# One-core three-branch block: where the first and third branch's merges take up their first gates

## The chip, the cores and the metric
The kernel runs on one core of one Trainium2 chip, as one launch. The metric is device time in microseconds (us). The three runs of the kernel before took 2590.54, 2594.08 and 2594.62 us, so its median is 2594.08 us.

## The reference, cut to what matters
The reference is a block of two layers on 512 tokens (256 of context, 256 of the sequence) with 1024 features, and then a second block of two layers on the 256 tokens of the sequence. Only the first block is touched. In each of its layers three branches read the same normalised input h: an mLSTM (a), a differential attention (b) and a Fourier mix (c). Each has a gate of its own, and their gated outputs are summed:

```
for l in (0, 1):
    h   = modulate(rmsnorm(x), c)
    y_a = rmsnorm(mlstm(h)) * sigmoid(o) * silu(z)      # 4 heads, 256 columns each
    y_b = attention(h) * silu(bz)
    y_c = fourier_mix(cu) * silu(cz)                    # 4 groups of 256 columns
    m   = sigmoid(mg_a) * (y_a @ w_a_out) + sigmoid(mg_b) * (y_b @ w_b_out) \
        + sigmoid(mg_c) * (y_c @ w_c_out)               # mg_* = h @ w_in[...]
    x   = x + gate * (m @ w_out)
```

`fourier_mix` of a group transforms its 256 columns (first transform) and then along its 256 tokens (second transform), each as a product with tables of cosines and sines. In layer 0 all 512 tokens go through; in layer 1 only the last 256 are needed at the end.

## The kernel before, in words
**Layout.** Activations lie with features on the 128 partitions and tokens along the free axis, in 8 tiles. Each tile is kept as a high part (rounded to fp32r) and a low part (the rest): `HYh` and `HYl`, whose first half is the layer's input H and whose second half is the branch's output YB. Weights are split in the same way, `wh` and `wl`. A projection of 128 output columns is 8 tiles times 3 matmuls (high*high, high*low, low*high), 24 matmuls in one PSUM bank, on 512 tokens in layer 0 and on 256 in layer 1.

**Weights.** They come in units of 256 columns, in a fixed order, one DMA each into a ring `raw` of 2. ScalarE copies a unit to `wh` in two pieces (L1308, L1309), VectorE subtracts to give `wl` in two pieces (L1846, L1848). `wh` and `wl` are rings of 2 as well: the conversion of a unit waits until TensorE has used the unit two before it, and the DMA after next waits for the conversion.

**Order.** There is no scheduler. Each engine has a program written by hand (`tensor_program`, `scalar_program`, `vector_program`, `pool_program`, `sync_program`) and works through it in that order. Waits are on semaphores that count named events, such as `("c_uc", l, g, 0)`; an event is set by one engine's instruction and waited for in another's program.

**Third branch.** `branch_c` runs over four groups g. TensorE projects `c_u` (L492), projects `c_z`, does the second transform of the group before (`output(g - 1)`, event `c_f2`, banks 6 and 7) and then the first transform of this group (`c_f1`, banks 2 and 3). ScalarE copies bank 2 to `c_uc[0]`, VectorE copies bank 3 to `c_uc[1]` (L1838); the second transform reads both. ScalarE copies its odd part, VectorE combines even and odd (L1827), GpSimd multiplies by `c_z` (L2561), ScalarE writes the high part of YB (`gated`), GpSimd the low part (L2561). Behind the loop over the groups stands `output(3)`, with no projection ahead of it.

**Merge.** `merge(l, br)`, for the first and third branch, makes eight gates (projections of H, banks 0 and 1) and eight values (projections of YB, banks 2 and 3). Unit 0 holds the weights of gates 0 and 1, unit j those of value j-1 and gate j+1, unit 7 values 6 and 7. TensorE takes them as gate 0, gate 1, value 0, gate 2, value 1, gate 3 and so on. In the first branch the turn of the last head's output (`outputs_turned(l, 3)`) stands between gates 0 and 1. ScalarE applies tanh or sigmoid to a gate on its way to `TMG` (L1298); VectorE multiplies by the value. In layer 0 a small product for the modulation (`ada_unit`, `raw` times `sc`) stands behind each unit of the first branch's merge.

Gate 0 writes bank 0, so it waits until ScalarE has read `c_z` of the last group out of that bank. Value 0 writes bank 2 and reads YB, its last two tiles last (k = 6, 7).

Of the kernel before, what the change touches and what calls it, by code (L numbers as in the profile page):

```python
# [198 lines left out]
def program(nc, wpk, xin, memt, vec, tabs, tabs2, rpb, out):  # L199
# [10 lines left out]
    with ctx:  # L210
# [69 lines left out]
        def bank(b):  # L280
            return PS[:, b]
# [43 lines left out]
        H = hy(0, 8, 512)  # L325
# [162 lines left out]
        def tensor_program(P):  # L488
# [190 lines left out]
            def h_ready(l):  # L679
                return lambda k: (dve_step, ("H", l, k)) if k % 2 == 0 else (pool_step, ("H", l, k))  # L680

            def merge(l, br):
                t0, N = lay(l)

                def gate(u, c, j):
                    if j >= 2:
                        P.wait_ge(act_step, ("m_gate", l, br, j - 2))
                    elif br == "a":
                        P.wait_ge(dve_step, ("a_z", l, 3, j))
                    else:  # L690
                        P.wait_ge(act_step, ("c_z", l, 3, j))
                    proj_t(bank(j % 2)[:, 0:N], u, c, 128, H, h_ready(l), 0, 8, t0, N, ("m_gate", l, br, j),
                           *([("unit", u)] if c and j < 8 and j else []))

                def value(u, c, j):
                    if j >= 2:
                        P.wait_ge(dve_step, ("m_value", l, br, j - 2))
                    elif br == "a":
                        P.wait_ge(dve_step, ("a_h", l, 3, 3))
                    else:  # L700
                        P.wait_ge(act_step, ("c_uc", l, 3, 0))
                        P.wait_ge(dve_step, ("c_uc", l, 3, 1))
                    proj_t(bank(2 + j % 2)[:, 0:N], u, c, 128, YB, lambda k: ((dve_step if br == "a" else pool_step), ("YB", l, br, k)), 0, 8, t0, N,
                           ("m_value", l, br, j), *([("unit", u)] if c else []))

                for j in range(8):
                    u = place["m_" + br, 8 * l + j]
                    if j == 0:
                        gate(u, 0, 0)
                        if br == "a":  # L710
                            outputs_turned(l, 3)
                        gate(u, 128, 1)
                    else:
                        value(u, 0, j - 1)
                        if j < 7:
                            gate(u, 128, j + 1)
                        else:
                            value(u, 128, 7)
                    if (q := ada_at(l, br, j)) is not None:
                        ada_unit(q)  # L720
                        if q > NADA:
                            ada_turn(q - 1)
# [145 lines left out]
            def branch_c(l):  # L868
                t0, N = lay(l)
                ready = lambda k: (dve_step, ("H", l, k)) if k % 2 == 0 else (pool_step, ("H", l, k))  # L870
                seqs = (0, 1) if l == 0 else (1,)
                P.wait_ge(pool_step, "half")

                def output(g):

                    P.wait_ge(act_step, ("c_uc", l, g, 0))
                    P.wait_ge(dve_step, ("c_uc", l, g, 1))
                    for kc in range(2):
                        if g:
                            P.wait_ge(dve_step, ("c_even", l, g - 1, kc))  # L880
                            P.wait_ge(act_step, ("c_odd", l, g - 1, kc))
                        for s in seqs:
                            for a, z, col in ((0, 129, 0), (129, 256, 256)):
                                for c in range(2):
                                    t = mm(bank(6 + kc)[:, 256 * s + a:256 * s + z], CS[:, c, col + 128 * kc:col + 128 * kc + 128],
                                           c_uc[:, c, s, a:z], c == 0, c == 1)
                        t.then_inc(*pe_step.mark(("c_f2", l, g, kc)))

                for g in range(4):
                    u = place["c_u", 4 * l + g]  # L890
                    for b in seqs:
                        P.wait_ge(act_step, ("c_z", l, g - 1, b) if g else ("m_gate", l, "b", 6 + b))
                        for i in range(2):
                            proj_k(bank(b)[:, 256 * i:256 * i + 256], u, H, ready, 8, 128 * (2 * b + i), ("c_u", l, g, b),
                                   *([("unit", u)] if b else []))
                    u = place["c_z", 4 * l + g]
                    for c in range(2):
                        if c in seqs:
                            P.wait_ge(act_step, ("c_u", l, g, c))
                        elif g == 0:  # L900
                            P.wait_ge(act_step, ("m_gate", l, "b", 6))
                        else:
                            P.wait_ge(act_step, ("c_z", l, g - 1, 0))
                        proj_t(bank(c)[:, 0:N], u, 128 * c, 128, H, ready, 0, 8, t0, N, ("c_z", l, g, c), *([("unit", u)] if c else []))
                    if g:
                        output(g - 1)
                    P.wait_ge(act_step, ("c_u", l, g, 1))
                    for c in range(2):
                        if g:
                            P.wait_ge(dve_step if c else act_step, ("c_uc", l, g - 1, c))  # L910
                        else:
                            P.wait_ge(dve_step, ("m_value", l, "b", 6 + c))
                        for s in seqs:
                            for t_ in range(2):
                                t = mm(bank(2 + c)[:, 256 * s:256 * s + 256], c_u[:, 2 * s + t_, 128 * c:128 * c + 128], CS[:, t_, 512:768],
                                       t_ == 0, t_ == 1)
                        t.then_inc(*pe_step.mark(("c_f1", l, g, c)))
                output(3)

            def project_out(l):  # L920
                t0, N = lay(l)
# [359 lines left out]
            ada_turn(NADA - 1)  # L1281
            for l in range(2):
                branch_a(l)
                merge(l, "a")
                branch_b(l)
                merge_b(l)
                branch_c(l)
                merge(l, "c")
                project_out(l)
            for l in range(2):  # L1290
                second_block(l)
# [4 lines left out]
        def scalar_program(A):  # L1296
# [107 lines left out]
                    A.wait_ge(projected, ("m_value", 0, "c", 7))  # L1404
                act(YB[0][:, 2 * h:2 * h + 2, t0:512], a_z[:, :, 0:N], ACT.Copy, ("YB", l, "a", 2 * h))

            def merge(l, br):
                t0, N = lay(l)

                def gate(j):  # L1410
                    A.wait_ge(projected, ("m_gate", l, br, j))
                    if j >= 3:
                        if br == "a":
                            A.wait_ge(dve_step, ("m_value", l, br, j - 3))
                        else:
                            A.wait_ge(pool_step, ("m_sum", l, br, j - 3))
                    elif br == "c":
                        A.wait_ge(pe_step, ("b_t", l, *B_ALL[l][-1]))
                    f, x = (ACT.Tanh, 0.5) if br == "a" else (ACT.Sigmoid, 1.0)
                    act(TMG[:, 512 * (j % 3):512 * (j % 3) + N], bank(j % 2)[:, 0:N], f, ("m_gate", l, br, j), scale=x)  # L1420

                def merged(ks):
                    for k in ks:
                        A.wait_ge(projected, ("m_gate", l, br, 7))
                        A.wait_ge(pool_step, ("m_sum", l, br, k))
                        act(H[0][:, k, t0:512], Y[:, k, t0:512], ACT.Copy, ("merged", l, k))

                for j in range(8):
                    if j == 0:
                        gate(0)  # L1430
                        if br == "a":
                            outputs_high(l, 3)
                        gate(1)
                    elif j < 7:
                        gate(j + 1)
                    if j == 7 and br == "c":
                        merged(range(6))
                    used("m_" + br, 8 * l + j)
                if br == "c":
                    merged((6, 7))  # L1440
# [103 lines left out]
            def branch_c(l):  # L1544
                t0, N = lay(l)
# [10 lines left out]
                def gated(g):  # L1556
# [2 lines left out]
                        A.wait_ge(projected, ("m_value", l, "b", 7))  # L1559
                    act(YB[0][:, 2 * g:2 * g + 2, t0:512], c_y[:, :, 0:N], ACT.Copy, ("YB", l, "c", 2 * g))  # L1560

                for g in range(4):
                    for b in seqs:
                        A.wait_ge(projected, ("c_u", l, g, b))
# [17 lines left out]
                    act(c_uc[:, 0, s0:], v2(2)[:, s0:], ACT.Copy, ("c_uc", l, g, 0))  # L1582
                    if g:
                        gated(g - 1)
                output(3)
                gated(3)

            def project_out(l):
                if l == 0:
# [211 lines left out]
            for l in range(2):  # L1801
# [10 lines left out]
                    if l == 0 and k == 4:  # L1812
                        convert(converted[1])
                branch_a(l)
                merge(l, "a")
                branch_b(l)
                merge_b(l)
                branch_c(l)
                merge(l, "c")
                project_out(l)  # L1820
            for l in range(2):
                second_block(l)
# [1104 lines left out]
```

## Time and profile before
| | us |
|---|---|
| median of 3 runs (lowest, highest) | 2594.08 (2590.54, 2594.62) |
| the profiled execution: its own time | 2593.25 |
| its span, from the first to the last instruction | 2591.4 |
| TensorE busy (share of the span) | 2381.4 (92%) |
| VectorE busy | 1338.5 (52%) |
| ScalarE busy | 1018.7 (39%) |
| GpSimd busy | 257.1 (10%) |
| DMA: bytes, mean rate | 291.45 MB, 112 GB/s |
| mean granted TensorE clock | 0.954 |

The profile comes from one execution. Of its 2591.4 us TensorE computes in 2381.4; some 210 us are idle, in many short gaps. In a row of the timeline the bracket at the end gives the idle time of the engine just before the instruction and the instruction that ended it. A granted clock of 1.00 is 2.4 GHz and 0.50 is 1.2 GHz. Ends of matmuls are modelled, so their starts are the safer numbers.

### The profile page before, as it was taken

How to read it: one execution, taken by the hardware profiler on the slowest of the kernel's cores; microseconds unless marked ns; L12 is line 12 of the kernel's file. 1: busy time of each engine (PE TensorE's matmuls, PEld its weight loads, DVE VectorE, ACT ScalarE, POOL GpSimd, SP SyncE). 2: the span in 40 equal slices, each digit the busy share in tenths (PEclk: the TensorE clock that was granted, in tenths of full speed). 3: DMA queues.
4: the chain of work that ended last, by engine and by line, in shares of the span. 5: the costliest groups of instructions: out<-in, count | busy, mean ns of one | idle time of the engine just before them, and what ended most of it. 6: DMA issues, size and time to landing. Idle time of an engine off the chain costs nothing.

```text
span 2591.4 us, 38368 instructions
## 1 busy us (share of the span) xinstructions
PE 2381.4 (92%) x16176; PEld 2138.1 (83%) x16176; DVE 1338.5 (52%) x2735; ACT 1018.7 (39%) x1939; POOL 257.1 (10%) x264
## 2 busy tenths in 40 slices
PE   5999999999979999689999899978888999898998
PEld 3788879888768978579999889878677999767998
DVE  5444424677433223555457664366655555565654
ACT  2333322444422222234335353443444444454443
POOL 1000002222001111000022211200100110100110
PEclk7999999999999999889999999989998999898999
DMA  6211143111223112133242233353222544302444
GB/s 241 90 74 66 51 173 134 66 66 66 82 98 147 66 66 97 48 111 114 98 147 98 82 107 140 139 170 121 75 98 98 182 172 167 129 33 98 179 170 140
DMA packets 50412, 291.45 MB, mean 112 GB/s; under 512 B 8960, under 2 KB 13312, under 8 KB 19072
## 3 DMA queue, kind: packets, MB, share of 16 engines
q1 hardware_dynamic: 50240, 289.00, 30.8%
q8 instruction: 127, 2.08, 0.3%
q14 instruction: 45, 0.37, 0.0%
HBM read 286.89 MB, written 2.36 MB: 112 GB/s over the span
## 4 chain that ended last, share of the span: by engine, by line
PE 75%; DVE 14%; ACT 5%; DMA 2%; issue 1%; SPq 1%; POOL 1%; DVEq 0%; ACTq 0%; POOLq 0%
PE PS L492 73%; DVE wl L1846 3%; DVE wl L1848 2%; PE PS L496 2%; ACT wh L1308 2%; DMA raw<-in_wpk 2%; DVE TM L1827 2%; ACT TM L1298 1%; ACT TMG L1298 1%; DVE colS L1835 1%; DVE HYl L1835 1%; DVE TMG L1835 1%; DVE TM L1835 1%; ACT HYh L1298 1%; DVE colS L2287 1%
## 5 line engine op out<-in xcount | busy, mean ns | idle before, releaser
L492 PE MATMUL PS<-HYh,wh 128*128 128x256 f32 (+1 forms) x3000 | 961.3, 320 | 60.8 <-DVE HYl L1835 31.9
L492 PE MATMUL PS<-HYl,wh 128*128 128x256 f32 (+1 forms) x3000 | 944.9, 315 | 0.0
L492 PE MATMUL PS<-HYh,wl 128*128 128x256 f32 (+1 forms) x3000 | 943.6, 315 | 0.0
L1846 DVE TENSOR_TENSOR wl<-raw,wh 128x1280 fp32r<-128x1280 f32 (+2 forms) x254 | 368.6, 1451 | 636.8 <-ACT wh L1308 636.8
L492 PEld LDWEIGHTS PS<-HYh,wh 128*128 128x128 f32 x3000 | 585.8, 195 | 107.1 <-DVE HYl L1835 36.7
L492 PEld LDWEIGHTS PS<-HYh,wl 128*128 128x128 f32 x3000 | 585.5, 195 | 31.1
L492 PEld LDWEIGHTS PS<-HYl,wh 128*128 128x128 f32 x3000 | 586.6, 196 | 29.1
L1308 ACT ACTIVATE wh<-raw 128x1280 fp32r<-128x1280 f32 (+2 forms) x254 | 306.5, 1207 | 384.9 <-PE PS L492 245.2
L492 PE MATMUL PS<-wh,HYh 128*128 128x256 f32 x1458 | 423.9, 291 | 13.0 <-DVE HYl L1835 11.2
L492 PE MATMUL PS<-wh,HYl 128*128 128x256 f32 x1458 | 415.1, 285 | 0.0
L492 PE MATMUL PS<-wl,HYh 128*128 128x256 f32 x1458 | 415.0, 285 | 0.0
L1298 ACT ACTIVATE TM<-PS 128x512 f32<-128x512 f32 (+4 forms) x339 | 163.4, 497 | 566.7 <-PE PS L492 436.1
L492 PEld LDWEIGHTS PS<-wh,HYh 128*128 128x128 f32 x1458 | 281.9, 193 | 18.0 <-DVE HYl L1835 12.0
L492 PEld LDWEIGHTS PS<-wl,HYh 128*128 128x128 f32 x1458 | 281.9, 193 | 0.4
L492 PEld LDWEIGHTS PS<-wh,HYl 128*128 128x128 f32 x1458 | 281.6, 193 | 0.1
L492 PE MATMUL PS<-TM 128*128 128x128 f32 (+6 forms) x992 | 222.6, 404 | 32.0 <-ACT colC L1298 12.2
L1848 DVE TENSOR_TENSOR wl<-raw,wh 128x768 fp32r<-128x768 f32 (+2 forms) x254 | 248.2, 977 | 0.0
L1309 ACT ACTIVATE wh<-raw 128x768 fp32r<-128x768 f32 (+2 forms) x254 | 206.8, 814 | 0.0
L492 PEld LDWEIGHTS PS<-TM 128*128 128x128 f32 (+2 forms) x992 | 148.3, 197 | 67.4 <-ACT colC L1298 13.4
L2561 POOL TENSOR_TENSOR HYl<-TM,HYh 128x256 fp32r<-128x256 f32 (+2 forms) x60 | 59.9, 1000 | 682.5 <-ACT HYh L1298 682.5
L1298 ACT ACTIVATE TMG<-PS 128x512 f32<-128x512 f32 (+2 forms) x122 | 53.9, 442 | 160.9 <-PE PS L492 147.0
L1298 ACT ACTIVATE TMG<-PS,colS 128x512 f32<-128x512 f32 (+1 forms) x104 | 62.0, 602 | 82.8 <-DVE colS L1831 82.5
(178 smaller groups left out, 1803.0 us busy)
## 6 DMA issues: line engine op xcount, KB each, us to landing
raw<-in_wpk SPq DMA_DIRECT2D x235, 1024.0 KB, 4.8
raw<-in_wpk SPq DMA_DIRECT2D x32, 704.0 KB, 4.0
TM<-in_wpk SPq DMA_DIRECT2D x4, 1024.0 KB, 18.0
X<-in_xin SPq DMA_DIRECT2D x1, 2048.0 KB, 9.9
Y<-in_wpk SPq DMA_DIRECT2D x2, 1024.0 KB, 23.6
Y<-bias_d SPq DMA_DIRECT2D x4, 512.0 KB, 9.7
raw<-in_wpk SPq DMA_DIRECT2D x3, 512.0 KB, 4.7
T<-in_tabs SPq DMA_DIRECT2D x1, 1216.0 KB, 14.7
```

The source lines that it names most:

```text
L492: return P.x.matmul(o, l, r, start=start, stop=stop)
L496: return P.x.transpose(o, i, ident[0:p, 0:p])
L1298: return A.x.activation(o, i, f, **kw).then_inc(*act_step.mark(*events))
L1308: A.x.activation(wh[:, s, 0:c], raw[:, r, 0:c], ACT.Copy).then_inc(*hi_split.mark((u, 0)))
L1309: A.x.activation(wh[:, s, c:n], raw[:, r, c:n], ACT.Copy).then_inc(*hi_split.mark((u, 1)))
L1827: return D.x.tensor_tensor(o, a, b, op).then_inc(*dve_step.mark(*events))
L1835: return D.x.scalar_tensor_tensor(out=o, in0=a, scalar=s, in1=b, op0=op0, op1=op1).then_inc(*dve_step.mark(*events))
L1846: D.x.tensor_tensor(wl[:, s, 0:c], raw[:, r, 0:c], wh[:, s, 0:c], ALU.subtract).then_inc(*lo_split.mark())
L1848: D.x.tensor_tensor(wl[:, s, c:n], raw[:, r, c:n], wh[:, s, c:n], ALU.subtract).then_inc(*lo_split.mark(u))
L2287: D.x.reduce_max(mx, src, AX).then_inc(*dve_step.mark())
L2561: return G.x.tensor_tensor(o, a, b, op).then_inc(*pool_step.mark(*events))
```

## The change: what it does, and the diff
On TensorE, `branch_c` no longer ends with `output(3)`. It returns `output`, and `merge` calls it as `last(3)` between gate 0 and gate 1, as it already did with the turn in the first branch. In both merges gate 2 now stands ahead of value 0, in unit 1; from unit 2 on the order is value j-1, gate j+1 as before. The event that frees a unit goes with the last projection of it, so in unit 1 it is now value 0's. ScalarE's program takes gate 0 ahead of `output(3)` and `gated(3)`. VectorE's, GpSimd's and the DMA queue's programs are as they were.

```diff
--- before.py
+++ after.py
@@ -679,20 +679,19 @@
             def h_ready(l):
                 return lambda k: (dve_step, ("H", l, k)) if k % 2 == 0 else (pool_step, ("H", l, k))
 
-            def merge(l, br):
+            def merge(l, br, last):
                 t0, N = lay(l)
 
-                def gate(u, c, j):
+                def gate(u, c, j, *events):
                     if j >= 2:
                         P.wait_ge(act_step, ("m_gate", l, br, j - 2))
                     elif br == "a":
                         P.wait_ge(dve_step, ("a_z", l, 3, j))
                     else:
                         P.wait_ge(act_step, ("c_z", l, 3, j))
-                    proj_t(bank(j % 2)[:, 0:N], u, c, 128, H, h_ready(l), 0, 8, t0, N, ("m_gate", l, br, j),
-                           *([("unit", u)] if c and j < 8 and j else []))
-
-                def value(u, c, j):
+                    proj_t(bank(j % 2)[:, 0:N], u, c, 128, H, h_ready(l), 0, 8, t0, N, ("m_gate", l, br, j), *events)
+
+                def value(u, c, j, *events):
                     if j >= 2:
                         P.wait_ge(dve_step, ("m_value", l, br, j - 2))
                     elif br == "a":
@@ -701,21 +700,23 @@
                         P.wait_ge(act_step, ("c_uc", l, 3, 0))
                         P.wait_ge(dve_step, ("c_uc", l, 3, 1))
                     proj_t(bank(2 + j % 2)[:, 0:N], u, c, 128, YB, lambda k: ((dve_step if br == "a" else pool_step), ("YB", l, br, k)), 0, 8, t0, N,
-                           ("m_value", l, br, j), *([("unit", u)] if c else []))
+                           ("m_value", l, br, j), *events)
 
                 for j in range(8):
                     u = place["m_" + br, 8 * l + j]
                     if j == 0:
                         gate(u, 0, 0)
-                        if br == "a":
-                            outputs_turned(l, 3)
-                        gate(u, 128, 1)
+                        last(3)
+                        gate(u, 128, 1, ("unit", u))
+                    elif j == 1:
+                        gate(u, 128, 2)
+                        value(u, 0, 0, ("unit", u))
                     else:
                         value(u, 0, j - 1)
                         if j < 7:
-                            gate(u, 128, j + 1)
+                            gate(u, 128, j + 1, ("unit", u))
                         else:
-                            value(u, 128, 7)
+                            value(u, 128, 7, ("unit", u))
                     if (q := ada_at(l, br, j)) is not None:
                         ada_unit(q)
                         if q > NADA:
@@ -915,7 +916,7 @@
                                 t = mm(bank(2 + c)[:, 256 * s:256 * s + 256], c_u[:, 2 * s + t_, 128 * c:128 * c + 128], CS[:, t_, 512:768],
                                        t_ == 0, t_ == 1)
                         t.then_inc(*pe_step.mark(("c_f1", l, g, c)))
-                output(3)
+                return output
 
             def project_out(l):
                 t0, N = lay(l)
@@ -1281,11 +1282,10 @@
             ada_turn(NADA - 1)
             for l in range(2):
                 branch_a(l)
-                merge(l, "a")
+                merge(l, "a", lambda h: outputs_turned(l, h))
                 branch_b(l)
                 merge_b(l)
-                branch_c(l)
-                merge(l, "c")
+                merge(l, "c", branch_c(l))
                 project_out(l)
             for l in range(2):
                 second_block(l)
@@ -1404,7 +1404,7 @@
                     A.wait_ge(projected, ("m_value", 0, "c", 7))
                 act(YB[0][:, 2 * h:2 * h + 2, t0:512], a_z[:, :, 0:N], ACT.Copy, ("YB", l, "a", 2 * h))
 
-            def merge(l, br):
+            def merge(l, br, last):
                 t0, N = lay(l)
 
                 def gate(j):
@@ -1428,8 +1428,7 @@
                 for j in range(8):
                     if j == 0:
                         gate(0)
-                        if br == "a":
-                            outputs_high(l, 3)
+                        last(3)
                         gate(1)
                     elif j < 7:
                         gate(j + 1)
@@ -1559,6 +1558,10 @@
                         A.wait_ge(projected, ("m_value", l, "b", 7))
                     act(YB[0][:, 2 * g:2 * g + 2, t0:512], c_y[:, :, 0:N], ACT.Copy, ("YB", l, "c", 2 * g))
 
+                def last(g):
+                    output(g)
+                    gated(g)
+
                 for g in range(4):
                     for b in seqs:
                         A.wait_ge(projected, ("c_u", l, g, b))
@@ -1582,8 +1585,7 @@
                     act(c_uc[:, 0, s0:], v2(2)[:, s0:], ACT.Copy, ("c_uc", l, g, 0))
                     if g:
                         gated(g - 1)
-                output(3)
-                gated(3)
+                return last
 
             def project_out(l):
                 if l == 0:
@@ -1812,11 +1814,10 @@
                     if l == 0 and k == 4:
                         convert(converted[1])
                 branch_a(l)
-                merge(l, "a")
+                merge(l, "a", lambda h: outputs_high(l, h))
                 branch_b(l)
                 merge_b(l)
-                branch_c(l)
-                merge(l, "c")
+                merge(l, "c", branch_c(l))
                 project_out(l)
             for l in range(2):
                 second_block(l)
```

On TensorE, at the end of the third branch in layer 1 (`TM,T` of 129 and 127 columns is the second transform of group 3, `HYh,wh` and so on a projection of 24 matmuls; `...` stands for rows of it that repeat):

```order
 L492 MATMUL PS<-T,TM 128x256 x4
+L492 MATMUL PS<-HYh,wh 128x256
+L492 MATMUL PS<-HYl,wh 128x256
+L492 MATMUL PS<-HYh,wl 128x256
...
 L492 MATMUL PS<-TM,T 128x129 x2
 L492 MATMUL PS<-TM,T 128x127 x2
 L492 MATMUL PS<-TM,T 128x129 x2
 L492 MATMUL PS<-TM,T 128x127 x2
-L492 MATMUL PS<-HYh,wh 128x256
-L492 MATMUL PS<-HYl,wh 128x256
-L492 MATMUL PS<-HYh,wl 128x256
```

The 24 matmuls of gate 0 moved from behind the second transform to a place between the first transform (`T,TM`) and it. In layer 0 the same happens with 512 columns. The exchange of gate 2 and value 0 does not show in these names, since both are projections.

On ScalarE, at the same place in layer 1 (`TMG` is a gate, `TM` of 127 columns the odd part of the second transform, `HYh` of 2x256 the high part of YB, `wh` a conversion):

```order
 L1298 ACTIVATE HYh<-TM 128x2x256
+L1298 ACT_TABLE_LOAD
+L1298 ACTIVATE TMG<-PS 128x256
 L1298 ACTIVATE TM<-PS 128x127 x2
 L1298 ACTIVATE HYh<-TM 128x2x256
-L1298 ACT_TABLE_LOAD
-L1298 ACTIVATE TMG<-PS 128x256 x2
-L1308 ACTIVATE wh<-raw 128x1280
-L1309 ACTIVATE wh<-raw 128x768
 L1298 ACTIVATE TMG<-PS 128x256
+L1308 ACTIVATE wh<-raw 128x1280
+L1309 ACTIVATE wh<-raw 128x768
```

The table load and gate 0 moved ahead of the odd copies and of YB's last high part; gate 1 and the conversion of unit 2 keep their places behind these.

## Rows read from the trace of the kernel before

**Rows 1.** The page's part 1: busy us (share), instructions, by engine.
```profile
PE 2381.4 (92%) x16176; PEld 2138.1 (83%) x16176; DVE 1338.5 (52%) x2735; ACT 1018.7 (39%) x1939; POOL 257.1 (10%) x264
```

**Rows 2.** Waits of PE: waiting line <- awaited line: us in total, times, longest.
```profile
PE PS L492 <- DVE TM L1838: 9.5, 2, 4.8
```

**Rows 3.** Timeline, layer 0, end of third branch: start, us, instruction [idle before <-releaser].
```profile
922.48 1.09 ACT L1298 ACTIVATE TM<-PS 128x512 f32<-128x512 f32 x2 [2.36 <-POOL TM L2561]
927.03 0.68 DVE L1838 COPY TM<-PS 128x512 f32<-128x512 f32 x1
927.86 5.44 PE L492 MATMUL PS<-TM,T 128*128 128x129 f32 x32 [4.70 <-DVE TM L1838]
933.06 0.48 PE L492 MATMUL PS<-HYh,wh 128*128 128x512 f32 x1
937.18 2.40 POOL L2561 TENSOR_TENSOR HYl<-TM,HYh 128x1024 fp32r<-128x1024 f32 x1 [1.17 <-ACT HYh L1298]
938.63 0.39 PE L492 MATMUL PS<-HYh,wh 128*128 128x512 f32 x1
944.07 0.39 PE L492 MATMUL PS<-HYh,wh 128*128 128x512 f32 x1
```

**Rows 4.** Timeline, layer 1, end of the third branch and its merge.
```profile
1639.76 0.38 ACT L1298 ACTIVATE TM<-PS 128x256 f32<-128x256 f32 x1 [1.55 <-POOL TM L2561]
1643.02 0.95 DVE L1848 TENSOR_TENSOR wl<-raw,wh 128x768 fp32r<-128x768 f32 x1
1643.89 0.42 DVE L1838 COPY TM<-PS 128x256 f32<-128x256 f32 x1
1644.45 3.77 PE L492 MATMUL PS<-TM,T 128*128 128x129 f32 x16 [4.82 <-DVE TM L1838]
1650.69 1.28 ACT L1298 ACT_TABLE_LOAD   x1
1650.75 1.28 POOL L2561 TENSOR_TENSOR HYl<-TM,HYh 128x512 fp32r<-128x512 f32 x1 [0.74 <-ACT HYh L1298]
1651.10 0.28 PE L492 MATMUL PS<-HYh,wh 128*128 128x256 f32 x1
1651.98 0.38 ACT L1298 ACTIVATE TMG<-PS 128x256 f32<-128x256 f32 x1
1653.98 0.28 PE L492 MATMUL PS<-HYh,wh 128*128 128x256 f32 x1
1657.16 0.95 DVE L1848 TENSOR_TENSOR wl<-raw,wh 128x768 fp32r<-128x768 f32 x1
1659.74 0.28 PE L492 MATMUL PS<-HYh,wh 128*128 128x256 f32 x1
```

**Rows 5.** Windows: stretch, us, PE busy (x), PEclk, DMA share, GB/s.
```profile
554.53:555.53 1.00, 1.00 (x8) 1.00 0.74 147
915.97:919.54 3.57, 3.57 (x34) 1.00 0.00 0
927.86:933.06 5.20, 5.20 (x32) 0.67 0.62 205
1644.45:1647.87 3.42, 3.42 (x16) 0.50 0.72 285
```

**Rows 6.** Timeline: a wait in the second branch, layer 0.
```profile
554.53 0.39 PE L492 MATMUL PS<-wh,HYh 128*128 128x256 f32 x1 [1.83 <-DVE HYl L1835]
```

**Rows 7.** Timeline, first branch's merge, layer 0 (first two) and layer 1.
```profile
318.28 1.23 DVE L1827 TENSOR_TENSOR HYl<-TM,HYh 128x1024 fp32r<-128x1024 f32 x1 [1.13 <-ACT HYh L1298]
322.55 0.50 PE L492 MATMUL PS<-HYh,wh 128*128 128x512 f32 x1
1280.07 1.11 PE L496 MATMUL PS<-T,TM 128*128 128x128 f32 x4 [2.85 <-ACT TM L1298]
1282.40 0.69 DVE L1827 TENSOR_TENSOR HYl<-TM,HYh 128x512 fp32r<-128x512 f32 x1 [0.70 <-ACT HYh L1298]
1284.86 0.28 PE L492 MATMUL PS<-HYh,wh 128*128 128x256 f32 x1
```

## The prediction, made before the changed kernel ran
> **What bounds the kernel now.** I read the busy shares first, then TensorE's waits, then the timeline of all engines around the two waits that the change touches, last the granted clock there. TensorE computes for 92% of the span [rows 1], so a change pays only by shortening an idle stretch of TensorE, or by letting its matmuls run at the higher clock. The list of waits has one entry that belongs to this place alone: twice TensorE waits for VectorE's copy L1838, 9.5 us together, 4.8 the longest [rows 2]. These are the second transforms of group 3, one in each layer, at 927.86 after 4.70 us and at 1644.45 after 4.82 us of idle time [rows 3, 4]. The other groups have the projections of the next group ahead of their second transform; the last group has nothing.
>
> Why the copy is late matters. In layer 1 it starts at 1643.89, right behind the low part of a weight conversion (1643.02 + 0.95) [rows 4]. VectorE's queue sets the moment, not TensorE's. Moving a gate on TensorE doesn't move the copy, and it ends where it ended: 927.71 in layer 0 (927.03 + 0.68), 1644.31 in layer 1 (1643.89 + 0.42) [rows 3, 4].
>
> The wait has a second cost. The 32 matmuls of a second transform in layer 0 take 3.57 us at clock 1.00 (group 2) and 5.20 us behind the wait, at 0.67; in layer 1 the 16 take 3.42 us at 0.50 [rows 5], where half of 3.57, 1.79, would do. TensorE had been idle for over 4.6 us before both.
>
> **Third branch, layer 0.** Gate 0 may start when the first transform is done, at 927.86 - 4.70 = 923.16, and when ScalarE has read the first of the two `c_z` banks. The two reads together take 922.48 to 923.57 [rows 3]; the first is over at about 923.1 (half of it), 923.57 at the latest. I take 923.2. A gate at full clock is 5.44 us, from 938.63 to 944.07 [rows 3], so it ends at 928.64. By then the copy has been there for 0.9 us, and the second transform follows without a wait, 3.57 us: 932.21. There gate 1 begins. Before it began at 938.63. Gain 6.42 us: 4.70 of wait, 1.63 of slow clock, 0.1 of gate 0's own slower start.
>
> **Third branch, layer 1.** A gate is 2.88 us (1651.10 to 1653.98), about half as long, while the wait is as long as in layer 0. The first transform ends at 1644.45 - 4.82 = 1639.63, but bank 0 is read until 1640.14 (1639.76 + 0.38) [rows 4]: gate 0 starts at 1640.2 and ends at 1643.08. The copy still ends at 1644.31, so the second transform starts at 1644.45 as before. Some 1.4 us of wait stay, and 0.6 in front of the gate. Is the clock high behind them? At 554.53 it was 1.00 behind 1.83 us of idle time that stood between long work [rows 5, 6], so I take 1.79 us for the transform: 1646.24, where gate 1 began at 1651.10 before. Gain 4.86 us: 2.88 of wait filled, 1.63 of clock and 0.35 of gate 0's slow start (1647.87 to 1651.10 is 3.23, not 2.88). Bounds: with the clock low the transform takes 3.42 and gate 0 alone is gained, 2.88.
>
> **Gate 2 ahead of value 0, third branch.** It puts back the cover that gate 0 took away. Between the second transform and the tiles k = 6 of value 0 there were gates 0 and 1 and six eighths of value 0; now there are gates 1 and 2 and the same six eighths, 2.75 projections. In layer 1 that is 7.92 us, and the low part of YB was written 4.16 us after the transform's end (1652.03 - 1647.87) [rows 4], so 3.8 us are spare. In layer 0 it is 14.96 against 6.52 (939.58 - 933.06) [rows 3]. Cost 0. Without the exchange layer 1 would have 5.04 us, still enough.
>
> The weights of unit 2 are tighter. Their low part ended 4.13 us after gate 1 did (1658.11 - 1653.98), and TensorE needed them 5.76 us after it, at 1659.74 [rows 4]; 1.63 spare. That stays if ScalarE is free when gate 1 ends, since in its queue YB's last high part comes first. That part was over at 1650.69 (the table load followed), 2.82 us after the transform; now at 1646.24 + 2.82 = 1649.06, and gate 1 ends at 1646.24 + 2.88 = 1649.12. ScalarE is free just in time, and 1.63 us cover an error. Cost 0, bounds 0 and -0.5.
>
> **ScalarE's moved instructions.** Table load and gate 0 (1.28 and 0.38 us [rows 4]) now stand ahead of the odd copies. The table load has no wait of its own and can run behind the YB part of group 2, before gate 0 ends. If it ran only behind the gate's end at 1643.08, both would be over at 1644.74; the first odd copy is wanted when the first half of the transform is done, 1644.45 + 0.9 = 1645.35. Cost 0. The Trainium skill, "ScalarE: Activation LUTs", section "What ACT_TABLE_LOAD costs", gives 2.66 us for a switch of tables, 1.28 for the load and 1.38 for draining. The trace agrees with the first number, but gate 0 starts at 1651.98, 0.01 us behind the load, so no draining shows; with the page's sum the odd copy would be 0.8 us late, inside the 3.8 us spare, and the forecast would be the same.
>
> **First branch.** Only gate 2 and value 0 change places. They pay if value 0 waits for YB. In layer 0 YB's low part ends at 319.51 and value 0 starts at 322.55 or later; in layer 1 it ends at 1283.09 and value 0 starts at 1284.86 [rows 7]. Nothing is hidden that wasn't. The wait of 2.85 us at 1280.07 stands ahead of the turn, between gates 0 and 1, where nothing is moved. Unit 1 ends at the same moment in either order, so conversions and DMAs keep their times. Gain and cost 0, bounds -0.5 and +0.3.
>
> **Sum.** 6.42 + 4.86 = 11.28, less 0.1 for starts, is 11.2 us. The profiled execution took 2593.25 us; it would take 2582.05. The median of the runs shown is 0.83 higher, so the forecast for a median is 2582.9, rounded 2583. All that follows in the program moves up as a whole.
>
> **Rivals.**
> 1. The wait comes back whole. If gate 0 finds another wait as long as the one for the copy, only the order changes: 2591 to 2594 us. For it: bank 0 is freed late, by ScalarE behind a wait for GpSimd [rows 3, 4]. Against: this read is over at 1640.14, and unit 0's weights were converted before unit 1's, which were done at 1643.97; VectorE works in order, and between the two lies all of group 2's output. 6%.
> 2. The clock falls in layer 1 all the same. Then the gain there is 2.88, not 4.86, and the time 2583 + 2 = 2585. For it: two idle pieces, 0.6 and 1.4 us, close together, and behind the single 2.85 us at 1280.07 four turns took 1.11 us [rows 7], 0.28 each on average where back-to-back matmuls of a gate start every 0.12 (2.88 / 24). The Trainium skill, "TensorE: Matmul & The Clock Gate", section "Part 1: The HAM clock gate", holds that idleness brings the low clock and activity the high one, and that where the change falls differs between runs; by that rule this case is open in layer 1 and closed in layer 0, where no idle time is left. Against: 1.83 us left it high [rows 5, 6], and 2.88 us of work lie between the pieces. 14%.
> 3. The covers are thinner than worked out, and value 0 or unit 2 waits in layer 1 for 1 to 3 us: 2584 to 2586. For it: ScalarE is free only 0.06 us ahead of gate 1's end. Against: 1.63 and 3.8 us to spare. 5%.
> 4. Slower than before. One mechanism can do it: in layer 1's merge the clock falls in the remaining 1.4 us and stays low. At 0.50 the transform took 1.9 times as long, so a projection would take some 5.5 us, and the 15 still to come would lose 39 us, 2622 in all. A low stretch costs about half its length; it decides once it lasts some 22 us longer than the one of before. Against: gate 0 of before lost only 0.35 us, so the clock was back soon after 1647.87, under unbroken work as here. 3%.
>
> **How the numbers follow.** Forecast 72%, rivals 6, 14, 5 and 3%. A measurement of this kernel tells a change from none from about 0.2%, 5.2 us. The forecast and rivals 2 and 3 are faster by more: 91%; rival 1 is the same: 6%; rival 4 slower: 3%. For the range, the runs of before lie between 3.5 us below and 0.5 above their median, so the median after may well lie up to 3.5 below 2583 from that alone. Rivals 2 and 3 add 2 to 3 us above it. With the bounds of the small terms: 2579 to 2587. Outside it lie rivals 1 and 4 and the edges of the spread, under 20%.
>
> **What would show it.** In the profile after, the wait for L1838 should be gone in layer 0 and be about 1.4 us in layer 1. The second transform should take 3.57 us in layer 0 at clock 1.00, and 1.79 in layer 1. From the end of the first transform to the start of gate 1 I expect 9.1 us in layer 0 (15.5 before) and 6.6 in layer 1 (11.5 before). No wait for `HYl` or `wl` should stand in the merge, and in the first branch's merges the same turns should wait, 1.1 and 2.85 us. I'd be wrong in kind if a wait for weights stands ahead of value 1, or if a gain shows in the first branch; wrong in size if the transform of layer 1 takes 3.4 us.

## The result, and the profile after
The changed kernel took 2577.65 us (median of 4 runs, 2576.19 to 2580.28), the kernel before 2594.35 us (4 runs, 2590.54 to 2594.87). The ratio is 0.9947, with a 95% interval of 0.9933 to 0.9962, or some 13.8 us (9.9 to 17.4) less. The forecast was 2583, range 2579 to 2587: faster as forecast, and by somewhat more than the 11.2 us of the sum. The median itself lies 1.35 us below that range. The ratio, taken on the 2594.08 us that the forecast started from, gives 2580.3 (2576.7 to 2584.2), and five more runs of the same kernel had a median of 2580.42; both lie inside. The profiled execution took 2580.28 us, its span 2578.5 us, against 2593.25 and 2591.4: 12.9 us.

Busy time of each engine in the profile after, to be set beside [rows 1]:

```profile
PE 2379.7 (92%) x16176; PEld 2135.0 (83%) x16176; DVE 1339.7 (52%) x2735; ACT 1018.7 (40%) x1939; POOL 257.2 (10%) x264
```

TensorE's busy time fell by 1.7 us only; its idle time fell by 11. That split must not be read as the worth of the clock: ahead of 794 us, where the third branch hasn't begun, TensorE was busy for 729.67 us before and 734.32 after in the same time. The table of stretches below puts this right. The list of TensorE's waits, after, has this line where [rows 2] had 9.5 us in two waits:

```profile
PE PS L492 <- DVE TM L1839: 1.1, 1, 1.1
```

The timeline after, layer 0 (start, us, instruction, idle before and releaser), answers to [rows 3]:

```profile
923.03 0.50 PE L492 MATMUL PS<-HYh,wh 128*128 128x512 f32 x1
926.93 0.69 DVE L1839 COPY TM<-PS 128x512 f32<-128x512 f32 x1
928.61 3.73 PE L492 MATMUL PS<-TM,T 128*128 128x129 f32 x32
932.10 0.48 PE L492 MATMUL PS<-HYh,wh 128*128 128x512 f32 x1
```

Gate 0 starts at 923.03, the copy runs beside it at the old time, the transform follows without a bracket, and gate 1 starts at 932.10 where it was 938.63. Layer 1 answers to [rows 4]. All of it is 6.05 us earlier here, so 1640.20 is 1646.25 on the clock of the rows before:

```profile
1633.73 0.66 ACT L1298 ACTIVATE TM<-PS 128x256 f32<-128x256 f32 x2 [1.55 <-POOL TM L2562]
1634.16 0.39 PE L492 MATMUL PS<-HYh,wh 128*128 128x256 f32 x1 [0.57 <-ACT TM L1298]
1636.99 0.95 DVE L1849 TENSOR_TENSOR wl<-raw,wh 128x768 fp32r<-128x768 f32 x1
1637.09 1.28 ACT L1298 ACT_TABLE_LOAD   x1
1637.86 0.42 DVE L1839 COPY TM<-PS 128x256 f32<-128x256 f32 x1
1638.38 0.39 ACT L1298 ACTIVATE TMG<-PS 128x256 f32<-128x256 f32 x1
1638.42 2.02 PE L492 MATMUL PS<-TM,T 128*128 128x129 f32 x16 [1.13 <-DVE TM L1839]
1640.20 0.37 PE L492 MATMUL PS<-HYh,wh 128*128 128x256 f32 x1
1642.97 1.30 POOL L2562 TENSOR_TENSOR HYl<-TM,HYh 128x512 fp32r<-128x512 f32 x1 [0.74 <-ACT HYh L1298]
1646.34 0.95 DVE L1849 TENSOR_TENSOR wl<-raw,wh 128x768 fp32r<-128x768 f32 x1
1648.92 0.28 PE L492 MATMUL PS<-HYh,wh 128*128 128x256 f32 x1
```

The reader sees the gate between two short waits, 0.57 us for the read of bank 0 and 1.13 us for the copy, which still stands right behind the conversion on VectorE. Unit 2's low part is ready at 1647.29 (1646.34 + 0.95), and value 1, which needs it, starts at 1648.92, so 1.6 us were to spare. The granted clock of both transforms after (stretch, us, PE busy, PEclk, DMA share, GB/s) stands against 0.67 and 0.50 in [rows 5]:

```profile
928.61:932.10 3.49, 3.49 (x34) 1.00 0.70 291
1638.42:1640.20 1.78, 1.78 (x17) 1.00 0.60 156
```

In the first branch's merges only gate 2 and value 0 changed places. The turns wait 1.08 and 2.85 us, where they waited 1.09 (first line, from before) and 2.85 [rows 7]:

```profile
315.05 1.09 PE L496 MATMUL PS<-T,TM 128*128 128x128 f32 x8 [1.09 <-ACT TM L1298]
```

```profile
314.74 1.09 PE L496 MATMUL PS<-T,TM 128*128 128x128 f32 x8 [1.08 <-ACT TM L1298]
1273.86 1.11 PE L496 MATMUL PS<-T,TM 128*128 128x128 f32 x4 [2.85 <-ACT TM L1298]
```

In layer 0, 18.64 us lie between the turn and the second `raw` times `sc` product, before and after. In layer 1 it is 4.79 us from the turn to the projection behind gate 1 before and 4.90 after.

**Where the 12.9 us came from.** Four instructions of TensorE stand in every one of these programs with a short wait in front of them: the `raw` times `sc` product near 794, a projection near 1025, the last `c_u` projection near 1624 and the first output projection near 1699. Their starts cut the span into five stretches, I to V, each in us. II and IV hold the third branch's end and its merge in layers 0 and 1. I and III hold the first branch's merges, V holds nothing that was changed.

These are the cuts, of before and then of after:

```profile
794.12 1.07 PE L492 MATMUL PS<-raw,sc 128*32 128x256 f32 x16 [0.93 <-DVE ada L1831]
1025.38 0.50 PE L492 MATMUL PS<-HYh,wh 128*128 128x512 f32 x1 [0.91 <-DVE HYl L1827]
1624.35 0.39 PE L492 MATMUL PS<-wh,HYh 128*128 128x256 f32 x1 [0.85 <-ACT TM L1298]
1699.15 0.39 PE L492 MATMUL PS<-HYh,wh 128*128 128x256 f32 x1 [2.53 <-DVE HYl L1827]
```

```profile
794.00 1.07 PE L492 MATMUL PS<-raw,sc 128*32 128x256 f32 x16 [0.45 <-DVE ada L1832]
1018.96 0.50 PE L492 MATMUL PS<-HYh,wh 128*128 128x512 f32 x1 [0.91 <-DVE HYl L1828]
1618.30 0.38 PE L492 MATMUL PS<-wh,HYh 128*128 128x256 f32 x1 [0.84 <-ACT TM L1298]
1688.32 0.39 PE L492 MATMUL PS<-HYh,wh 128*128 128x256 f32 x1 [2.53 <-DVE HYl L1828]
```

| kernel | I | II | III | IV | V | span |
|---|---|---|---|---|---|---|
| before | 794.12 | 231.26 | 598.97 | 74.80 | 892.25 | 2591.4 |
| changed | 794.00 | 224.96 | 599.34 | 70.02 | 890.18 | 2578.5 |
| changed, again | 795.58 | 224.98 | 595.42 | 70.01 | 890.01 | 2576.0 |
| gate 0 only | 793.92 | 225.01 | 598.86 | 70.02 | 890.19 | 2578.0 |
| exchange only | 796.21 | 231.64 | 598.95 | 74.82 | 892.08 | 2593.7 |
| third branch only | 799.13 | 224.97 | 596.38 | 70.01 | 890.01 | 2580.5 |
| layer 0 only | 792.53 | 224.92 | 598.68 | 74.50 | 892.57 | 2583.2 |
| filler, 18 | 796.76 | 232.46 | 598.12 | 75.61 | 891.25 | 2594.2 |
| filler, 9 | 794.53 | 229.73 | 597.93 | 72.90 | 890.71 | 2585.8 |
| copy first | 791.17 | 225.91 | 598.19 | 69.21 | 891.02 | 2575.5 |
| both | 791.22 | 224.92 | 598.99 | 68.66 | 891.31 | 2575.1 |
| two gates | 795.44 | 227.41 | 599.77 | 70.60 | 893.08 | 2586.3 |

II fell by 6.30 us and IV by 4.78, together 11.08. V gave 2.07 more, I and III 0.12 and -0.37. II and IV repeat within 0.1 us in the four profiles that have gate 0 ahead in both layers (changed, again, gate 0 only, third branch only). The order of before was profiled once; the kernel with the exchange alone, whose waits are the same, has 0.38 us more in II, all of it in a slower second transform (5.57 us at clock 0.62, against 5.20 at 0.67). I spreads over 8 us and III over 4, and the edits don't sort them: changed and again, the same kernel, differ by 1.6 and 3.9. So the experiments are read by II and IV first, and by the times second.

The windows of II and IV show what kind of time was gained (stretch, us, PE busy, PEclk, DMA share, GB/s), before and then after:

```profile
794.12:1025.38 231.26, 225.61 (x1258) 0.99 0.25 91
1624.35:1699.15 74.80, 67.45 (x539) 0.95 0.38 141
```

```profile
794.00:1018.96 224.96, 224.01 (x1259) 1.00 0.26 94
1618.30:1688.32 70.02, 65.79 (x538) 1.00 0.43 151
```

TensorE's busy time fell by 1.60 and 1.66 us, 3.26 together, and its idle time by 4.70 and 3.12, 7.82 together. The first is the clock's part of the 11.08 us, the second the part of the filled wait.

### The profile page after: what moved, and what is told of

Read it like the earlier page. It is cut to its first block, busy times and chain, and to the rows that moved or that the text cites. A ratio compares the mean times of both kernels' runs of the same rounds, so it can differ in the third digit from the quotient of the medians.

```text
span 2578.5 us, 38373 instructions
## 1 busy us (share of the span) xinstructions
PE 2379.7 (92%) x16176; PEld 2135.0 (83%) x16176; DVE 1339.7 (52%) x2735; ACT 1018.7 (40%) x1939; POOL 257.2 (10%) x264
## 4 chain that ended last, share of the span: by engine, by line
PE 76%; DVE 14%; ACT 5%; DMA 2%; issue 1%; SPq 1%; POOL 1%; DVEq 0%; ACTq 0%; POOLq 0%
PE PS L492 74%; DVE wl L1847 2%; DVE wl L1849 2%; PE PS L496 2%; ACT wh L1308 2%; DMA raw<-in_wpk 2%; DVE TM L1828 2%; ACT TM L1298 1%; ACT TMG L1298 1%; DVE colS L1836 1%; DVE HYl L1836 1%; DVE TM L1836 1%; ACT HYh L1298 1%; DVE TMG L1836 1%; DVE colS L2288 1%
## 5 line engine op out<-in xcount | busy, mean ns | idle before, releaser
L492 PE MATMUL PS<-wh,HYh 128*128 128x256 f32 x1458 | 424.8, 291 | 13.0 <-DVE HYl L1836 11.2
```

The costliest lines, as they stand in the source:

```text
L492: return P.x.matmul(o, l, r, start=start, stop=stop)
```

## The experiments
**The changed kernel again** (no edit).

> The changed kernel once more. Theory P (the two waits for the copy are filled and the second transforms run at the high clock): 11.2 us by the local sum, with what the clock does later 11 to 14, so 2580 to 2583 us beside a before of 2594. Rival R (the other runs of the changed kernel, 13 to 18 us faster than before, show something that the profiled one lacks): 15 to 18 us again, 2576 to 2579.

Measured: 2580.42 us (5 runs), ratio 0.9951 (0.9937 to 0.9965), 13.8 us less than a before of 2594.23. II and IV are the same to 0.02 us. The median speaks against rival R (15 to 18 us), though the interval, 9.1 to 16.3 us, reaches into it. The profile shows where a shorter execution is shorter: this one is 2.5 us below the first of the same kernel, II and IV are the same, and III (3.9 less) and I (1.6 more) make the difference. So what the shorter runs have more is not in the edited stretches.

**Gate 0 alone.**

```diff
-                    elif j == 1:
-                        gate(u, 128, 2)
-                        value(u, 0, 0, ("unit", u))
```

> Third branch's gate 0 ahead of the last second transform, but gate 2 behind value 0 as before, in both merges. Theory P: the cover behind the transform in layer 1 is 5.04 us against a chain of 4.16, so nothing waits and the whole gain stays: within 1 us of the changed kernel. Rival S (gate 2's place is needed): value 0 waits for YB in layer 1, 1 to 3 us are lost, and a wait for HYl stands behind gate 1.

Measured: 2579.96 us, ratio 0.9948 (0.9936 to 0.9961); II 225.01, IV 70.02. The whole gain is there without the exchange, with no new wait behind the transform. Theory P holds, rival S falls.

**The exchange alone.**

```diff
-                merge(l, "c", branch_c(l))
+                branch_c(l)(3)
+                merge(l, "c", lambda h: None)
```

The same on ScalarE.

> Only the exchange of gate 2 and value 0, in both merges; the last second transform stands ahead of gate 0 as before. Theory P: 0, within 2 us of before, and the waits of 4.70 and 4.82 us are there. Rival S: 2 to 5 us faster than before, the part of the measured gain that the two waits don't explain.

Measured: 2593.37 us (11 runs), ratio 0.9997 (0.9988 to 1.0007); II 231.64, IV 74.82, neither shorter than before, and the wait list has the old line. The exchange gains nothing here.

```profile
PE PS L492 <- DVE TM L1841: 9.5, 2, 4.8
```

**The third branch alone.**

```diff
-                    elif j == 1:
+                    elif j == 1 and br == "c":
```

> The changed kernel with the first branch's merge as before: the whole change in the third branch alone. Theory P: equal to the changed kernel within 1 us, since the first branch's merge hid everything before. Rival S1 (the exchange in the first branch gains): 2 to 4 us slower than the changed kernel.

Measured: 2577.62 us (6 runs, 2571.44 to 2582.30), ratio 0.9940 (0.9925 to 0.9955); II 224.97, IV 70.01. Equal to the changed kernel in both stretches, and its times overlap with that kernel's.

**A filler in the wait, 18 products.** Its result is read by nobody.

```diff
+                for _ in range(18):
+                    mm(bank(4)[:, 0:256], CS[:, 0, 512:640], CS[:, 0, 512:768])
                 output(3)
```

> The kernel before, with 18 matmuls of tables into the unused bank 4 between the last first transform and the last second transform, whose result nobody reads; they fill about 4.1 us of each wait and move no other work. Theory P (idle time ahead of the transform costs 1.63 us of slow clock in each layer, and 0.1 and 0.35 us in the gate behind): the waits stay, now 0.6 to 0.8 us long behind the filler, the transforms start at the same times, take 3.57 and 1.79 us, and 3.5 to 3.9 us are gained. Rival Q (the slow transform is not due to the idle time): 0 gained, transforms at 5.20 and 3.42 us.

Measured: 2594.53 us, ratio 1.0012 (1.0003 to 1.0021), a miss, and mine: each product is two matmuls of the array (36 stand in the timeline), so the 18 took 7.8 us and outlasted the wait. II and IV grew by 1.20 and 0.81 us. Still, the transforms behind it ran at the high clock:

```profile
933.41:936.90 3.49, 3.49 (x33) 1.00 0.14 56
1650.24:1651.95 1.71, 1.71 (x18) 1.00 0.52 216
```

**The filler at half the size** (`range(9)`).

> The filler again at half the size: 9 table products, which take 3.9 us (the 18 of the run before took 7.8 and so delayed the transforms by 3.1 us). They lie wholly within the waits of 4.7 and 4.8 us. Theory P (idle time ahead of the transform costs it the high clock): the transforms start as long behind the first transforms as before, take 3.5 and 1.7 us instead of 5.2 and 3.4, and the stretches of the third branch are shorter by 1.7 to 1.9 us in layer 0 and by 1.7 to 2.1 in layer 1, 3.4 to 4.0 together, hardly to be told in the times alone. Rival Q: no shorter.

Measured: 2585.60 us, ratio 0.9972 (0.9962 to 0.9983). II fell by 1.53 us, a little less than the 1.7 to 1.9 expected, and IV by 1.90 against before, 3.43 together, though TensorE does strictly more work and the order of all else is that of before:

```profile
928.38 3.81 PE L492 MATMUL PS<-TM,T 128*128 128x129 f32 x32 [0.82 <-DVE TM L1840]
1642.30 2.02 PE L492 MATMUL PS<-TM,T 128*128 128x129 f32 x16 [0.94 <-DVE TM L1840]
```

Their granted clock is 1.00 both times (3.56 and 1.78 us). So the idle time, not the place in the program, costs the transform its clock, and that is about 3.4 of the 11.1 us, close to the 3.26 us by which TensorE's busy time fell in II and IV of the changed kernel. The rest of the 7 us in the times stands in stretches that hold no edit (V 1.5, III 1.0) and in the spread.

**Layer 0 alone.**

```diff
-                merge(l, "c", branch_c(l))
+                last = branch_c(l)
+                if l:
+                    last(3)
+                merge(l, "c", last if l == 0 else lambda h: None)
```

The same on ScalarE.

> The changed kernel with gate 0 ahead of the last second transform in layer 0 only; in layer 1 the transform stands ahead of gate 0 as before. Theory P: 6.4 to 6.5 us faster than before, the wait of 4.82 us and the transform of 3.42 us in layer 1 are as before. Rival Q: over 9 us or under 4.

Measured: 2584.97 us (11 runs), ratio 0.9977 (0.9968 to 0.9987), 6.0 us less by the ratio; II 224.92 (6.34 less), IV 74.50. In layer 1 the wait of 4.82 us is back. What the clock costs behind it isn't quite what it was: the transform took 2.90 us at clock 0.60, where 3.42 at 0.50 were expected, and gate 0 behind it 3.42 us at 0.84, where it took 3.23 at 0.90.

**The copy ahead of the conversion,** kernel before otherwise. On VectorE, and likewise on ScalarE:

```diff
-                    used("c_z", 4 * l + g)
+                    if g < 3:
+                        used("c_z", 4 * l + g)
                     D.wait_ge(pe_step, ("c_f1", l, g, 1))
...
                     cp(c_uc[:, 1, s0:], v2(3)[:, s0:], ("c_uc", l, g, 1))
+                    if g == 3:
+                        used("c_z", 4 * l + g)
```

> The kernel before, with ScalarE's and VectorE's copies for the last group put ahead of the conversion of the next unit on their queues; TensorE's order is as before. Theory P (the copy is late because it stands behind a conversion, not because of TensorE): the wait ahead of the transform falls from 4.70 to about 1.0 us in layer 0 and from 4.82 to about 1.25 in layer 1, set by ScalarE's copy behind the reads of c_z, the transforms run at the high clock, and 10 to 12 us are gained, 2582 to 2584. Rival Q (the later conversion makes TensorE wait for weights in the merge): a wait for wl of 0.5 us or more at unit 1, gain under 9.

Measured: 2579.41 us, ratio 0.9957 (0.9944 to 0.9969). The waits are 0.95 and 1.12 us, as expected, and now end with ScalarE's copy:

```profile
921.17 3.84 PE L492 MATMUL PS<-TM,T 128*128 128x129 f32 x32 [0.95 <-ACT TM L1298]
1631.68 2.05 PE L492 MATMUL PS<-TM,T 128*128 128x129 f32 x16 [1.12 <-ACT TM L1298]
```

II and IV fell by 5.35 and 5.59 us, 10.94 together: almost the gain of the change, with TensorE's order untouched. The wait was made on VectorE's and ScalarE's queues. No wait for weights appeared. The row of before shows what the copy stood behind in layer 1:

```profile
1641.61 1.49 DVE L1846 TENSOR_TENSOR wl<-raw,wh 128x1280 fp32r<-128x1280 f32 x1 [2.74 <-ACT wh L1308]
```

The first transform was over at 1639.63. VectorE was idle for 2.74 us until 1641.61, since the next entry of its program, the conversion, waited for ScalarE's part of it. So 1.98 of the 4.26 us by which the copy came after its input were idle time of VectorE, the rest its work on the conversion. The run moved both engines' copies at once, so the share of each isn't shown.

**Both.**

> The changed kernel with the copies ahead of the conversion as well. Theory P: the remaining wait for the copy in layer 1, 1.13 us, is gone, nothing changes in layer 0, 1.1 us faster than the changed kernel in the profile, hardly to be told in the times. Rival Q (the later conversion makes TensorE wait): equal or slower, with a wait for wl.

Measured: 2576.55 us (5 runs, 2575.36 to 2578.89), ratio 0.9946 (0.9933 to 0.9958). The wait for the copy in layer 1 is gone, and none for `wl` came. II is 224.92 as in the changed kernel, IV 68.66, 1.36 less for the 1.1 expected. It is the shortest by the two stretches; the times don't tell it from the changed kernel.

**Two gates ahead,** and no exchange, so that value 0 stands right behind the transform. ScalarE's program is changed alike.

```diff
                         gate(u, 0, 0)
-                        last(3)
+                        if br == "a":
+                            last(3)
                         gate(u, 128, 1, ("unit", u))
-                    elif j == 1:
-                        gate(u, 128, 2)
-                        value(u, 0, 0, ("unit", u))
+                        if br == "c":
+                            last(3)
```

> Gates 0 and 1 of the third branch's merge both ahead of the last second transform, value 0 right behind it, gate 2 after value 0; first branch as before. That fills the remaining 1.1 us in layer 1 but takes away all cover between the transform and value 0 but its own first six tiles. Theory P (YB's low part ends 6.5 and 4.2 us after the transform, and 4.1 and 2.2 us of value 0 lie ahead of its tiles 6 and 7): the wait for the copy is gone, waits for HYl of about 2.4 us in layer 0 and 2.0 us in layer 1 stand inside value 0, the two stretches together are 2.5 to 4 us longer than in the changed kernel, 2582 to 2584 beside a before of 2594. Rival T (the chain behind the transform needs no cover): no such wait, 1 us faster than the changed kernel.

Measured: 2586.43 us (11 runs), ratio 0.9975 (0.9966 to 0.9984), 6.5 us less than a before of 2592.57. That is less than the 10 to 12 us expected. The wait for the copy is gone and these came in its place:

```profile
945.49 0.50 PE L492 MATMUL PS<-HYh,wh 128*128 128x512 f32 x1 [2.16 <-POOL HYl L2565]
1650.12 0.38 PE L492 MATMUL PS<-HYh,wh 128*128 128x256 f32 x1 [1.70 <-POOL HYl L2565]
```

II and IV are 3.03 us longer than in the changed kernel (2.45 and 0.58), as expected. The miss in the time is elsewhere: V is 2.90 us longer than in the changed kernel, with no edit in it, and why stays open. The chain behind the transform, which ends with YB's low part, is real and nearly as long as worked out (waits of 2.4 and 2.0 us were expected). Value 0's own first six tiles are not enough to cover it. With gate 1 added they are, as the kernel with gate 0 alone shows.

## Why the prediction was right
- **What bounds the place.** Right. The copy kept its time on VectorE, in layer 1 4.26 us after the end of the first transform before and 4.27 after, and moved only when its own queue was changed (the copy-first kernel).
- **Third branch, layer 0.** Forecast: gate 0 at 923.2, transform at 928.64, gate 1 at 932.21. Measured 923.03, 928.61, 932.10. From the end of the first transform to gate 1 it was 15.47 us before (923.16 to 938.63) and is 9.07 now, 6.40 less for a forecast of 6.42; all of stretch II gave 6.30. Two terms are off and cancel. The second transform took 3.49 us and not 3.57. Gate 0 took 5.58 us and not 5.44: the 0.1 us that the forecast put down to its slow start behind the low clock was not gained.
- **Third branch, layer 1.** Forecast: gate 1 at 1646.24; measured 1646.25 on the same clock. The waits of 0.6 and 1.4 us are 0.57 and 1.13, the transform was forecast at 1.79 us and took 1.78. The same distance went from 11.47 to 6.61 us, the forecast 4.86; all of stretch IV gave 4.78. Here too gate 0 was slower than forecast, 3.13 us for 2.88 at a granted clock of 1.00, and the wait for the copy took it up (1.13 instead of 1.4).
- **The clock's share.** Right for the transforms, too large for gate 0. Forecast were 1.63 us in each layer plus 0.1 and 0.35 in gate 0, 3.7 together. The transforms gave 1.71 and 1.64 (5.20 to 3.49, 3.42 to 1.78). Gate 0 gave nothing in layer 0 (5.57 us before, already at clock 1.00) and 0.10 in layer 1 (3.23 to 3.13). That is 3.4 together, and the half filler, which takes away most of the idle time alone, gave 3.43:

```profile
933.06:938.63 5.57, 5.57 (x27) 1.00 0.00 0
923.03:928.61 5.58, 5.58 (x26) 1.00 0.03 6
1634.16:1637.29 3.13, 3.12 (x24) 1.00 0.00 0
```

The first line is from before, the others from after. The sum hardly felt it, since in layer 1 the longer gate only filled more of the wait.

- **The exchange, third branch.** Cost 0 was right, and so was that layer 1 would do without it. Unit 2's weights had the 1.6 us to spare that were forecast.
- **ScalarE's moved instructions.** Cost 0 was right. The table load ended at 1638.37 and gate 0 was over at 1638.77, ahead of the odd copy at 1639.59.
- **First branch.** Right: 0 in layer 0, and 0.1 us longer in layer 1, where the forecast had bounds of -0.5 and +0.3.
- **Rivals.** Rivals 1 to 4 did not come. The one low clock that was feared, in layer 1, stayed away in all six kernels with gate 0 ahead there. Why two waits of 0.57 and 1.13 us with a gate between them leave the clock high isn't shown; the forecast leaned on one wait of 1.83 us that had done so, and gave the rival 14%.
- **The sum.** 11.2 us against 11.08 in the two stretches. What it lacked is stretch V, 2.07 us. The forecast said that all that follows moves up as a whole. It did not quite: the projection at the start of V has the same wait of 2.53 us in front, and behind it the clock fell before and stayed high after. First the kernel before, then the changed one, both for 6.68 us from the end of that wait:

```profile
1699.15:1705.83 6.68, 6.68 (x43) 0.74 0.65 251
```

```profile
1688.32:1695.00 6.68, 6.68 (x55) 1.00 0.69 239
```

From there to the next common wait it was 17.05 us before and 15.56 after, so 1.5 of the 2.07 us are this one fall. The forecast had no term for it, and what decides it stays open (see the last section), so that V added to the gain is luck. The remaining 0.6 us are not settled.

## What to carry to other kernels
When the bottleneck engine waits for a copy, look first at what stands ahead of the copy on its own queue: moving the two copies past one conversion in each layer gave 10.9 us here, about as much as reordering the bottleneck engine. Put independent work into a wait up to its length and no more, and count what chain starts behind the delayed step. An idle stretch costs more than its length if the clock falls with it; here the transforms behind the waits of 4.7 and 4.8 us took 1.1 to 2.0 us more than at the high clock (2.90 to 3.42 for 1.79, 5.20 and 5.57 for 3.57).

## What the runs showed of the hardware that was not expected
**One wait, two clocks.** The wait of 2.53 us (2.52 once) at the start of stretch V stands in all twelve profiles. In the 6.68 us behind it the granted clock was 1.00 in six of them (changed, again, gate 0 only, third branch only, copy first, half filler) and 0.74 to 0.77 in the other six (before, exchange only, layer 0 only, filler, both, two gates). So the length of a gap of this size does not settle whether the clock falls to 1.2 GHz. The four profiles with gate 0 ahead in both layers and no other edit around it (the first four named) fell alike, though their starts differ by 4.5 us; what decides stays open. The Trainium skill, "TensorE: Matmul & The Clock Gate", section "Part 1: The HAM clock gate", says that the point of transition depends on phase and differs between runs. The traces agree that the gap alone does not fix it. That it differs between runs of one program doesn't show in them: the two profiles of the changed kernel were alike, and so were the two that differ from it only in the place of gate 2.

**A slow subtraction.** In the copy-first kernel the second part of a conversion on VectorE took 2.05 us instead of 0.95. It lay beside GpSimd's write of YB's low part, from 1634.11 to 1635.46, which began 0.12 us ahead of it:

```profile
1634.23 2.05 DVE L1851 TENSOR_TENSOR wl<-raw,wh 128x768 fp32r<-128x768 f32 x1
```

```profile
1634.11 1.35 POOL L2567 TENSOR_TENSOR HYl<-TM,HYh 128x512 fp32r<-128x512 f32 x1 [3.51 <-ACT HYh L1298]
```

In the kernel before the same two met in the other order. VectorE began at 1643.02 and took its 0.95 us [rows 4], and GpSimd, 0.16 us behind it, took 1.91 us instead of the 1.3 that such a write took elsewhere:

```profile
1643.18 1.91 POOL L2561 TENSOR_TENSOR HYl<-TM,HYh 128x512 fp32r<-128x512 f32 x1 [3.51 <-ACT HYh L1298]
```

Both read two tensors in SBUF. Each time the one that began second was the slower. That they hold each other up is a reading of these lines; no run took one away. A wait for either doesn't show on TensorE here.
